# First mixer's low-rank products: three fp32r terms on interleaved array rows instead of fp32 products

## The reference, cut to what matters

```python
r, k, v, xw, xa, xg = jnp.split(xm, RWKV_SPLITS, axis=-1)
w = -jax.nn.softplus(-(lp['rwkv_w0'] + jnp.tanh(xw) @ lp['rwkv_w2'])) - 0.5
a = jax.nn.sigmoid(lp['rwkv_a0'] + xa @ lp['rwkv_a2'])
g = jax.nn.sigmoid(xg) @ lp['rwkv_g2']
```

## Time and profile before

| what | value |
|---|---|
| three runs | 1351.08, 1352.9, 1353.68 us |
| median | 1352.9 us |
| profiled execution, its own time | 1353.87 us |
| span of its trace | 1352.1 us |
| PE busy | 1329.3 us (98%) |
| DVE busy | 855.8 us (63%) |
| ACT busy | 692.6 us (51%) |
| mean granted clock of PE | 0.997 |

### The profile page before, as it was taken

The page is one execution under the profiler, slowest core; times in us unless marked ns, Lnnn a source line. Parts: engine busy times, 40 slices in busy tenths (PEclk is TensorE's granted clock), DMA queues, the critical chain, the costliest instruction groups (busy, mean ns, idle before and its releaser), DMA issues.

```text
span 1352.1 us, 31424 instructions
## 1 busy us (share of the span) xinstructions
PE 1329.3 (98%) x12584; PEld 1289.2 (95%) x12584; DVE 855.8 (63%) x1327; ACT 692.6 (51%) x995; POOL 77.4 (6%) x113
## 2 busy tenths in 40 slices
PE   7999999999999999999999999999999999999997
PEld 7999999998988999999999999999888899999997
DVE  6656533898876756553376565349988766555533
ACT  7444423757655644443364444347466655454423
POOL 0000000200030100000010000001001310000001
PEclk9999999999999999999999999999999999999999
DMA  8544454322313644444454444443223244444541
GB/s 302 173 143 150 144 155 155 111 79 80 112 50 111 212 145 150 146 154 154 142 189 153 155 143 152 151 144 110 80 79 97 66 158 156 155 148 147 155 142 53
DMA packets 50768, 185.90 MB, mean 137 GB/s; under 512 B 5760, under 2 KB 6272, under 8 KB 50176
## 3 DMA queue, kind: packets, MB, share of 16 engines
q1 hardware_dynamic: 49104, 177.37, 41.3%
q10 hardware_dynamic: 1584, 7.35, 1.5%
HBM read 180.14 MB, written 4.56 MB: 137 GB/s over the span
## 4 chain that ended last, share of the span: by engine, by line
PE 86%; DVE 11%; issue 2%; ACT 1%; DMA 0%; DVEq 0%; ACTq 0%
PE ps L479 27%; PE ps L481 26%; PE ps L480 26%; DVE wl L1592 2%; DVE ar L1749 2%; PE ps L847 1%; DVE ar L1663 1%; PE ps L749 1%; PE ps L1035 0%; DVE raw L1967 0%; PE ps L817 0%; PE ps L1013 0%; PE ps L799 0%; DVE ar L1740 0%; DVE ar L1683 0%
## 5 line engine op out<-in xcount | busy, mean ns | idle before, releaser
L479 PE MATMUL ps<-xh,wh 128*128 128x320 f32 x1952 | 611.8, 313 | 9.0 <-DVE xl L1614 8.0
L1592 DVE TENSOR_TENSOR wl<-raw,wh 128x1024 fp32r<-128x1024 f32 x332 | 408.1, 1231 | 317.5 <-ACT wh L1186 317.1
L481 PE MATMUL ps<-xh,wl 128*128 128x320 f32 x1952 | 604.4, 310 | 0.0
L480 PE MATMUL ps<-xl,wh 128*128 128x320 f32 x1952 | 604.3, 310 | 0.0
L1186 ACT ACTIVATE wh<-raw 128x1024 fp32r<-128x1024 f32 x332 | 349.3, 1054 | 356.2 <-PE ps L481 339.1
L479 PEld LDWEIGHTS ps<-xh,wh 128*128 128x128 f32 x1952 | 367.5, 188 | 20.1 <-issue 9.0
L480 PEld LDWEIGHTS ps<-xl,wh 128*128 128x128 f32 x1952 | 367.7, 188 | 0.5
L481 PEld LDWEIGHTS ps<-xh,wl 128*128 128x128 f32 x1952 | 367.6, 188 | 0.0
L479 PE MATMUL ps<-hid_h,wh 128*128 (+1 forms) x704 | 217.5, 309 | 0.0
L480 PE MATMUL ps<-hid_l,wh 128*128 (+1 forms) x704 | 217.5, 309 | 0.0
L481 PE MATMUL ps<-hid_h,wl 128*128 (+1 forms) x704 | 217.5, 309 | 0.0
(11 more groups left out here) (290 smaller groups left out, 934.6 us busy)
## 6 DMA issues: line engine op xcount, KB each, us to landing
raw<-wts SPq DMA_DIRECT2D x332, 512.0 KB, 3.5
ms<-mst ACTq DMA_DIRECT2D x2, 1440.0 KB, 7.9
mout<-ms ACTq DMA_DIRECT2D x2, 1440.0 KB, 6.6
x<-xT SPq DMA_DIRECT2D x4, 320.0 KB, 4.9
yT<-x SPq DMA_DIRECT2D x4, 320.0 KB, 2.4
cs<-cst SPq DMA_DIRECT2D x1, 652.0 KB, 8.1
pr<-par ACTq DMA_DIRECT2D x1, 429.0 KB, 4.2
pr<-par ACTq DMA_DIRECT2D x1, 425.0 KB, 5.3
```

Source lines behind the costliest of these rows:

```text
L479: pe.matmul(out, a, rh, start=start, stop=False)
L480: pe.matmul(out, a, rl, start=False, stop=False)
L481: return pe.matmul(out, b, rh, start=False, stop=stop)
L1592: tt(wl[:, s, :], raw_of(layer, n), wh[:, s, :].bitcast(F32), ALU.subtract).then_inc(lo_ready.sem, 1)
```

## The change

It makes fp32r copies of the low-rank weights and of the activated tile, subtracts to get both remainders, and computes each low-rank product as three fp32r terms added up in PSUM. The 18 matmuls of a layer are ordered so that three neighbours lie on partitions 0 to 31, 32 to 63 and 64 to 127 and on banks 4, 6 and 2 (then 5, 7 and 3). The three `lora_mm` signals come with the last three matmuls. Two new ACT copies and two new DVE subtractions are added, and one more wait on DVE. The four new buffers share their space with `chain`, which is written later. The signals `bPi`, `rw_ops` and `kPi` share one semaphore in the order in which DVE gives them.

```diff
-    "rw_P": 1, "kk_rn": 1, "rb": 1, "rw_ops": 1, "kPi": 1, "bPi": 1, "bonus": 1,
+    "rw_P": 1, "kk_rn": 1, "rb": 1, "rw_keyed": ("bPi", "rw_ops", "kPi"), "bonus": 1,
...
+        with nc.sbuf_tensor("in_h", [128, TOK], F32R) as in_h, nc.sbuf_tensor("in_l", [128, TOK], F32R) as in_l, \
+                nc.sbuf_tensor("lora_h", [128, 2 * 128], F32R) as lora_h, nc.sbuf_tensor("lora_l", [128, 2 * 128], F32R) as lora_l:
+            pass
...
             def lora(layer):
                 on(pe, layer, "lora_in")
-                lo = P("lora", 0, 256)
-                for rows, bank in ((slice(0, 32), 4), (slice(32, 64), 6), (slice(64, 128), 2)):
-                    if bank == 2:
-                        on(pe, layer, in_read, RING)
-                    for p in range(2):
-                        ins = pe.matmul(ps[:, bank + p, 0:TOK], lo[rows, p * 128:p * 128 + 128], xm[rows, 6, :], start=True, stop=True)
-                    put(ins, "lora_mm")
+                on(pe, layer, in_read, RING)
+                terms = ((lora_h, in_h), (lora_h, in_l), (lora_l, in_h))
+                for p in range(2):
+                    for n, (weights, values) in enumerate(terms):
+                        for rows, bank in ((slice(0, 32), 4), (slice(32, 64), 6), (slice(64, 128), 2)):
+                            ins = pe.matmul(ps[:, bank + p, 0:TOK], weights[rows, p * 128:p * 128 + 128], values[rows, :],
+                                            start=n == 0, stop=n == len(terms) - 1)
+                            if p and n == len(terms) - 1:
+                                put(ins, "lora_mm")
...
                 norm_split(layer, 1, "nm")
+                st(act.activation(lora_h[:], P("lora", 0, 256), ACT.Copy))
                 rms(layer, 1)
...
-                say(act.activation(xm[64:128, 6, :], xm[64:128, 6, :], ACT.Sigmoid), "lora_in")
+                st(act.activation(xm[64:128, 6, :], xm[64:128, 6, :], ACT.Sigmoid))
+                st.settle()
+                say(act.activation(in_h[:], xm[:, 6, :], ACT.Copy), "lora_hi")
...
-                def rw_mix(lo, hi):
+                def rw_mix(lo, hi, between=None):
...
                     st(tt(seqs(xm[:, lo:hi], 0), seqs(rwp[:, lo:hi], 1, 0), seqs(rwp[:, lo:hi], 1, 1), ALU.subtract))
                     st.settle()
+                    if between:
+                        between()
...
+                def lora_low():
+                    on(ve, layer, "lora_hi")
+                    st(tt(lora_l[:], P("lora", 0, 256), lora_h[:].bitcast(F32), ALU.subtract))
+                    say(tt(in_l[:], xm[:, 6, :], in_h[:].bitcast(F32), ALU.subtract), "lora_in")
...
-                rw_mix(2, 4)
+                rw_mix(2, 4, lora_low)
```

More of the change, by code:

```diff
@@ L110 @@
 MIX_SIGNALS = {
-    "padded": ("pads", "rg_pads"), "xm": 7, "lora_in": 1, "lora_mm": 3, "sg": 2, "ra": 2,
+    "padded": ("pads", "rg_pads"), "xm": 7, "lora_hi": 1, "lora_in": 1, "lora_mm": 3, "sg": 2, "ra": 2,
     "rw_gc": 2, "shift_kept": 1, "kkraw": 2, "kk_sq": 1, "rkr": 2, "head_sums": ("kk_sum", "rk_sum", "gdn_sum"), "cum": 2, "prev": 1,
-    "rw_P": 1, "kk_rn": 1, "rb": 1, "rw_ops": 1, "kPi": 1, "bPi": 1, "bonus": 1,
+    "rw_P": 1, "kk_rn": 1, "rb": 1, "rw_keyed": ("bPi", "rw_ops", "kPi"), "bonus": 1,
     "rw_pairs": 2, "rw_pairs_read": 6,
@@ L127 @@
 }
-V_STEPS, A_STEPS, G_STEPS = 102, 51, 14 + 3 * 6
+V_STEPS, A_STEPS, G_STEPS = 102, 53, 14 + 3 * 6
 G_ALL = DEPTH * G_STEPS - 6
```

## The result

| | before | changed |
|---|---|---|
| median | 1353.04 us (4 runs, 1351.08 to 1353.68) | 1361.66 us (4 runs, 1359.12 to 1361.88) |
| ratio | 1 | 1.0065, 95% interval 1.0053 to 1.0077 |
| profiled execution | 1353.87 us | 1361.88 us |
| mean granted clock of PE | 0.997 | 0.992 |

The changed kernel is slower by 8.6 us, three times the 2.7 us of the forecast, and above its range (1357.8). The side was right, the size was not. One run each of e1_subs_only and e2_by_shape took 3325.02 and 2163.82 us, and both are left out of the ratios.

What follows compares the result with a forecast made beforehand. DVE was taken to bound each mixer from 254 to 328 us; per layer 0.74 us of subtractions plus 0.63 us of waiting gave 1.37, twice that 2.7, so 1352.9 + 2.7 = 1355.6 us, range 1352.7 to 1357.8.

Steps and rivals of the forecast that it cites:

- rival D: DVE part of the chain has unseen room, so PE's saving counts: 1350.2 us; chance 0.08 together with a lost fall.
- The copies on ACT and the moved waits: ACT's two new copies hidden in its idle time; waits on lora_hi, lora_in and in_read at cost 0.
- a forecast of 0.347: Low-rank products on PE: 12 steps of 0.147 plus 0.20 us for a change of shape, 4.2 us in all.
- rival A: Low-rank products: three neighbours run together, only DVE's subtractions count, 1.5 us, 1354.4 us; chance 0.30.
- B: Low-rank products: nothing overlaps, they take 5.0 us, chain shift 2.3 us a layer, 1357.4 us; chance 0.10.
- the low end: Low-rank products on PE with each group of three together: 6 x 0.147 = 0.88 us and one shape change, 1.2 us.
- 0.63 forecast: DVE's scan waits for ACT's `sg` sigmoids, starting at 265.60 instead of 264.97 us: 0.63 us more.
- The term for PE: PE 1.6 us later, 0.49 us of room at 293 us; the remaining 1.1 us lies under DVE's 1.37.
- rival C: PE's clock falls to the 1.2 GHz level once more, 1.5 us, about 1357 us in all; chance 0.10.
- PE's wait at 293 still for DVE: Expected sign: PE still waits for DVE's evacuation at 293 us, as in the kernel before (0.49 us).
- The forecast's own part: Chain shift on DVE per layer: 0.74 us of subtractions plus 0.63 us of waiting for `sg`, 1.37 us.
- the lost fall: The kernel before's clock fall in layer 1 can be absent, -1.5 us; chance 0.08 together with rival D.

Runs made afterwards that it cites:

- e1_subs_only: The changed kernel with the six fp32 products of the kernel before, keeping the ACT copies, DVE subtractions and wait on lora_hi: 1354.8 us, ratio 1.0012.
- e2_by_shape: The changed kernel with the same 18 matmuls ordered by shape, the 32-row ones first in pairs, then the 64-row ones: 1355.42 us, ratio 1.0016.
- e8_kk_on_act: The kernel before with the two kk scalings moved from DVE to ACT: 1351.96 us beside 1352.09, ratio 0.9996.
- e7_split: The changed kernel with its 18 matmuls cut in two by half of tile 5 (12 full matmuls): 1357.58 us, ratio 1.004.
- e5_half: The changed kernel with its order for the first 128 columns and by shape for the second: 1356.66 us, ratio 1.0036.
- e6_low_on_pool: The changed kernel ordered by shape, with both low-part subtractions on GpSimd instead of DVE: 1354.43 us, ratio 1.0014.
- after_again: The changed kernel itself, run again beside the later experiments: 1360.39 us, ratio 1.0069.
- e9_best_form: The changed kernel by shape, weights' remainder taken in DVE's wait for rstd, kk scalings on ACT: 1351.6 us beside 1352.09, ratio 1.0004.
- e3_fp32_twice: The kernel before with the six fp32 products computed twice, the first results overwritten: 1358.65 us, ratio 1.0048.
- e4_doubled: The changed kernel in its order, each of the 18 matmuls given twice in a row: 1366.0 us, ratio 1.0096.

## Why the prediction was wrong

**What held.** While the clock stays up, DVE bounds the stretch, by e1_subs_only (+0.71 us for subtractions of 0.74) and e8_kk_on_act (-0.37). A saving of PE is worth nothing then: shown by e2_by_shape, whose products take 0.4 us less than the fp32 ones of e1_subs_only and whose stretch is the same. That answers rival D. The copies on ACT and the moved waits cost nothing. The changes of shape drain PE: the step was 0.34 us for a forecast of 0.347, which rules out rival A, and the pairs of 32 rows ran together, which rules out B. The low-rank products took 4.6 us in layer 0 (260.88 to tile 5's 265.47) for 4.2; the last group ran at half clock already. (One sum of the prediction is off and changes nothing: by its own terms the low end is 0.88 + 0.20 = 1.1 us, not 1.2.) The page "TensorEngine Tiling (Array Packing)" of the Trainium skill, section Key Properties, says that a change of tiling mode drains the engine; the 0.16 us of idle ahead of each weight load of a new shape agrees with it. `sg` was late by more than DVE's arrival, with 0.41 us shown as waiting, for 0.63 forecast.

**What failed.** The term for PE: "So PE does not add." The step held PE's later work to its price at full clock, 1.6 us later with 0.49 us of room. The fall of the clock stood beside it as rival C, with a chance of 0.10, as one fall of 3.5 us for 1.5 us, "at 264 us some of it is covered by PE's room". It came in both layers, for 6.8 us in the first profile. Tile 5 starts at 265.47 and its evacuation had to wait until 271.79, 6.3 us; before, 24 such matmuls take 3.5 us. That overran the room, and DVE waited 1.09 us for the tile and 1.47 us for ACT behind it. The prediction expected "PE's wait at 293 still for DVE"; in both profiles of the changed kernel that wait is gone, and it is there in e1_subs_only, e2_by_shape and e7_split and in layer 0 of e5_half, which have no fall at the products (0.72, 0.70, 0.40 and 0.49 us). So PE bounded this part of the stretch, and its time did add. Of the 4.17 us in the stretch 0.74 are the subtractions, and by 1.2 to 1.5 us for the first 3.4 us at half clock and 1.5 for the second about 2.8 to 3.0 are the fall; the rest, 0.4 to 0.7 us, is what the draining costs beside it. The forecast's own part, 1.37 us a layer, stands against the 1.1 to 1.4 us found by leaving the falls out, so it may have been right; what was missing is the fall. Layer 1 has 1002.33 - 924.72 = 77.61 us, 4.09 more; both layers together make 8.3 us; the runs had 8.6, and the profiled executions differ by 8.0, since the rest of the program varies by a microsecond or two between executions. A part of that variation is the fall behind the inversions: 3.4 us, near 330 or 1000 us, it is in the profiles of the kernel before, of the changed kernel and of e1_subs_only to e6_low_on_pool, and absent in after_again, e7_split, e8_kk_on_act and e9_best_form. So the lost fall that the prediction named can come, but in the first profile of the changed kernel it did not, and it is no part of the 8.6.

**Why I gave it too little.** The rows of before showed a fall in one layer of two, behind a wait of half a microsecond and 2 us of small matmuls. The new order makes 4 us in which PE streams less than half of the time (12 steps of 0.34 us with 0.147 us of streaming in each). That row was the nearest for it, and should have been read as the likely case, not as a mishap; a fall also had to be priced where it lies, against the 0.49 us of room, and not as partly covered.

**What the runs settle of the fall, and what they don't.** With one change of shape inside the products instead of eleven it is gone (e1_subs_only, e2_by_shape), on few rows for 5.1 us it is absent (e3_fp32_twice), with the same steps cut by 1.8 us of full work it is absent (e7_split), and with half of them it is partly there (e5_half). So it comes with an unbroken run of draining steps. How much draining is too much stays open: doubling the streaming between the drains was not enough (e4_doubled), against my expectation. Why a fall lasts 3.4 us in one execution and 6.8 us in another is open as well. A run of the changed kernel without a fall was not seen, so the 1.1 to 1.4 us are an estimate and not a measurement.

## What to carry to other kernels

In these runs neighbouring matmuls on different rows of the array ran beside each other when they had the same shape (two of 32 rows), and not when they had unlike ones (32 rows and 64): each change cost 0.2 us. So group them by shape, and look twice at an order that alternates shapes in a dense stream. A stretch of PE that is "only" a few microseconds of drains is to be priced twice, once for its length and once for the clock, which here slowed the large products that follow. And before an exchange of PE time for vector time, look who waits for whom at the next meeting point: here PE waited for DVE, so each vector instruction cost its full time and the matmul time saved was worth nothing, until the fall turned that wait around.

## What was not expected of the hardware

GpSimd was no free helper for DVE: with a subtraction on POOL beside it, a 64-column multiply-add on DVE took 0.90 us instead of 0.28, and moving 0.74 us of work from DVE to POOL left the stretch longer by 0.87 us (254.73 to 329.12) instead of 0.71. And the fall of PE's clock varied between executions of one program: 3.4 us or 6.8 us at the products of layer 0.
